# Attention halves exchanged by DMA and rotated on GpSimd, keys copied twice out of PSUM, and one modulation unit folded earlier

## The reference

```python
def ffn_sublayer(x, shift, scale, gate, g_pre, g_post, w_in, w_out):
    h = modulate(rmsnorm(x, g_pre), shift, scale)
    a, b = jnp.split(h @ w_in, 2, axis=-1)
    h = (jax.nn.silu(a) * b) @ w_out
    return x + FFN_RES * gate * rmsnorm(h, g_post)

def apply_rope(x, cos, sin):
    x1, x2 = jnp.split(x, 2, axis=-1)
    return jnp.concatenate([x1 * c - x2 * s, x1 * s + x2 * c], axis=-1)

# attention, 16 query heads of 64 on 4 key heads; rope on the latent tokens alone
q, k, v = attn_project(h, w_qkv)           # context: softmax(q k) v with a sink
q, k = apply_rope(q, cos, sin), apply_rope(k, cos, sin)   # latent
# latent queries see a window of latent keys, the cached keys and the sink
```

## Time and profile before

| | us |
|---|---|
| median of 3 runs (lowest, highest) | 3009.32 (3008.97, 3010.02) |
| the profiled execution, whole | 3009.04 |
| its span, first to last instruction | 3007.2 |
| PE busy | 2956.2 (98%) |
| DVE busy | 2209.8 (73%) |
| ACT busy | 1152.2 (38%) |
| POOL busy | 561.6 (19%) |
| DMA rate | 172 GB/s mean |

### The profile page before, as it was taken

The page is one execution under the profiler, slowest core; times in us unless marked ns, Lnnn a source line. Parts: engine busy times, 40 slices in busy tenths (PEclk is TensorE's granted clock), DMA queues, the critical chain, the costliest instruction groups (busy, mean ns, idle before and its releaser), DMA issues.

```text
span 3007.2 us, 46610 instructions
## 1 busy us (share of the span) xinstructions
PE 2956.2 (98%) x18194; PEld 2749.9 (91%) x18194; DVE 2209.8 (73%) x2897; ACT 1152.2 (38%) x1966; POOL 561.6 (19%) x586
## 2 busy tenths in 40 slices
PE   7999999999999999999999999999999999999999
PEld 6999889999999998999899999979999999889998
DVE  6888678887987657888888576768888888775444
ACT  4222664223322424222422365553224222664222
POOL 1111112112111112111211144631112111211001
PEclk9999999999999999999999999999999999999999
DMA  9667445665665445766566443337675766333443
GB/s 306 211 215 215 140 91 187 212 211 170 217 213 175 119 128 173 223 213 199 178 213 201 134 118 104 95 99 231 211 216 181 220 212 197 112 81 114 127 128 95
DMA packets 589696, 517.76 MB, mean 172 GB/s; under 512 B 66773, under 2 KB 523046, under 8 KB 587686
## 3 DMA queue, kind: packets, MB, share of 16 engines
q1 hardware_dynamic: 588918, 514.53, 56.6%
q10 hardware_dynamic: 560, 0.25, 0.0%
...
## 4 chain that ended last, share of the span: by engine, by line
PE 91%; issue 4%; DVE 2%; POOL 1%; ACT 1%; DMA 1%; SPq 0%; DVEq 0%; POOLq 0%; another core or an unknown queue 0%; ACTq 0%
PE bank L1698 19%; PE bank L1700 19%; PE bank L1699 19%; PE bank L1752 9%; PE bank L1751 9%; PE bank L1750 9%; PE bank L1725 1%; PE bank L619 1%; PE bank L1715 1%; PE bank L644 1%; DVE h_hi L2266 1%; DMA ada_first<-w_ada 1%; DVE h_lo L2276 0%; POOL hg_kr L1497 0%; PE bank L1783 0%
## 5 line engine op out<-in xcount | busy, mean ns | idle before, releaser
L1698 PE MATMUL bank<-h_hi,w_hi 128*128 128x384 f32 x3328 | 1120.6, 337 | 0.0
L1700 PE MATMUL bank<-h_hi,w_lo 128*128 128x384 f32 x3328 | 1114.6, 335 | 0.0
L1699 PE MATMUL bank<-h_lo,w_hi 128*128 128x384 f32 x3328 | 1113.8, 335 | 0.0
L1947 ACT ACTIVATE w_hi<-raw 128x1024 fp32r<-128x1024 f32 x646 | 681.1, 1064 | 1020.1 <-PE bank L1700 481.6
L2109 DVE TENSOR_TENSOR w_lo<-raw,w_hi 128x1024 fp32r<-128x1024 f32 x648 | 810.4, 1274 | 310.9 <-ACT w_hi L1947 305.7
L1698 PEld LDWEIGHTS bank<-h_hi,w_hi 128*128 128x128 f32 x3328 | 625.3, 188 | 10.9 <-ACT tmp L1966 1.6
L1699 PEld LDWEIGHTS bank<-h_lo,w_hi 128*128 128x128 f32 x3328 | 625.4, 188 | 6.1
L1700 PEld LDWEIGHTS bank<-h_hi,w_lo 128*128 128x128 f32 x3328 | 625.2, 188 | 0.0
L2136 DVE SCALAR_TENSOR_TENSOR fold<-ada_raw,cond,fold 128x1024 f32<-128x1024 f32 x462 | 616.4, 1390 | 0.1
L2455 POOL TENSOR_TENSOR h_lo<-tmp,h_hi 128x384 fp32r<-128x384 f32 x176 | 250.2, 1421 | 1762.9 <-DVE h_hi L2180 1762.9
L1752 PE MATMUL bank<-w_hi,h_lo 128*128 128x512 f32 x1056 | 414.0, 392 | 0.0
...
## 6 DMA issues: line engine op xcount, KB each, us to landing
...
```

Source lines behind the costliest of these rows:

```text
L1698: mm(out, wh, h_hi[:, k, :], start=(k == 0), stop=False)
L1699: mm(out, wh, h_lo[:, k, :], start=False, stop=False)
L1700: last = mm(out, wl, h_hi[:, k, :], start=False, stop=(k == DC - 1))
L1947: A(w_hi[:, b % RING, :], raw[:, b % RAW, :], ACT.Copy).then_inc(w_hi_made, 1)
```

## The change

1. **Rope.** `rotate` is gone. SP copies the halves across partitions by DMA from `qkv` or `kd` into one of four buffers (`rope_tmp` twice, `rope_more` twice): two DMAs for a key head, four for a query chunk. POOL then multiplies the copy by the sine, the original by the cosine, and adds. DVE has no part in rope.
2. **Keys.** `dup` and the `take` of the key blocks are gone. ACT (block 0) and DVE (block 1) copy each key head twice from PSUM into `kd`, and the 128 context columns into `qkv`.
3. **Order.** The second value block moves to the end of the input blocks; its transposes run in the last loop step. Scores of chunk 2 and of chunk 7 stand earlier in their loop step. The exchanges stand in SP's list at blocks 8, 13 and 14 to 19.
4. **Unit 7** is folded in feed-forward 0, so that it holds six units in 22 steps of two or three slabs. Its sum is written at block 8 and spread at block 9 of the first attention, and its `mod_fold` stands in the loop step j = 0 there. The PE work and the loads of this unit in the attention are gone.
5. Slabs of feed-forward 0 are loaded two blocks later, its sums spread three blocks later; the constant table of an attention shrinks from 2048 to 1408 columns; the first eight slabs share semaphores in pairs.

```diff
-    QKV_CHUNKS = [DC, DC + 1, 0, DC + 2, DC + 3] + list(range(1, DC))
+    QKV_CHUNKS = [DC, DC + 1, 0, DC + 2] + list(range(1, DC)) + [DC + 3]
...
-    units_of = {0: (2, 7), 1: (7, 8), 2: (8, 13), 3: (13, 17), 4: (17, 17), 5: (17, 22), 6: (22, 26), 7: (26, 26),
+    units_of = {0: (2, 8), 1: (8, 8), 2: (8, 13), 3: (13, 17), 4: (17, 17), 5: (17, 22), 6: (22, 26), 7: (26, 26),
                 8: (26, 31), 9: (31, 36), 10: (36, 36), 11: (36, 36)}
     units_end = [units_of[s][1] for s in range(12)]
-    FOLD_F = 4
+    UNIT_STARTS = {5: (0, 4, 8, 12, 16, 20), 6: (0, 4, 8, 11, 15, 18, 21)}
...
     def sums_of(s):
         u0, u1 = units_of[s]
-        return {FOLD_F * (u - u0 + 1): u for u in range(u0, u1)}
+        return {unit_starts(s)[u - u0 + 1]: u for u in range(u0, u1)}
     def mods_of(s):
-        return {f + 2: u for f, u in sums_of(s).items()}
+        return {f + (4 if s == 0 else 2): u for f, u in sums_of(s).items()}
     def left_over(s):
...
     def spreads_of(s):
-        return {at_a(f) + 11: u for f, u in sums_of(s).items()}
+        return {at_a(f) + (14 if s == 0 else 11): u for f, u in sums_of(s).items()}
     def slabs_at(s, f):
-        u0, u1 = units_of[s]
-        u = u0 + f // FOLD_F
-        return [(u, 2 * (f % FOLD_F) + n) for n in range(2)] if u < u1 else []
+        starts = unit_starts(s)
+        for i, u in enumerate(range(*units_of[s])):
+            length = starts[i + 1] - starts[i]
+            if starts[i] <= f < starts[i + 1]:
+                per = -(-DC // length)
+                first = per * (f - starts[i])
+                return [(u, k) for k in range(first, min(first + per, DC))]
+        return []
...
-    attn_k = place("attn_k", [P, 5 * P + 2 * TS + KEYS], F32, x_end - 2 * D * 4)
+    attn_k = place("attn_k", [P, 2 * TS + KEYS], F32, x_end - 2 * D * 4)
...
+    rope_more = place("rope_more", [P, 2, TS], F32, x_end - 2 * TS * 4)
+    rope_of = [rope_tmp[:, 0, :], rope_tmp[:, 1, :], rope_more[:, 0, :], rope_more[:, 1, :]]
+    ROPE_BUFFERS = len(rope_of)
...
-    ROPE_ORDER = [("k", 0), ("k", 1), ("q", 0), ("k", 2), ("k", 3)] + [("q", j) for j in range(1, DC)]
-    FIRST_ROPES = 5
-    Q_AT = {j: ROPE_ORDER.index(("q", j)) for j in range(DC)}
+    TAKES = len(QKV_CHUNKS) - 2
+    FIRST_BLOCKS = 5
+    ROPE_ORDER = [("k", 0), ("k", 1), ("q", 0), ("k", 2), ("q", 1), ("k", 3)] + [("q", j) for j in range(2, DC)]
+    FIRST_ROPES = 6
+    ROPE_AT = {x: n for n, x in enumerate(ROPE_ORDER)}
+    KEY_SWAPS, QUERY_SWAPS = {8: (0, 1, 3), 13: (5,)}, {8: 2, 13: 4} | {b: b - 8 for b in range(14, 20)}
...
+    def rope_place(n):
         kind, i = ROPE_ORDER[n]
         return kd[:, i, TP:T] if kind == "k" else qkv[:, i, TP:T]
+    def swap_runs(n):
+        if ROPE_ORDER[n][0] == "k":
+            return [(0, 32, 96), (96, 0, 32)]
+        return [(to, to ^ 32, 32) for to in range(0, P, 32)]
...
+    def copy_keys(copy, c):
+        rows = [slice(0, HD), slice(HD, P)]
+        copy(qkv[:, DC + c, 0:TP], psum[c][:, 0:TP])
+        for x in range(2):
+            for half in rows:
+                last = copy(kd[half, 2 * c + x, :], psum[c][rows[x], 0:T])
+        return last
...
-            pe.wait_ge(rope_add, ROPE * a + Q_AT[j] + 1)
-            pe.wait_ge(k_dup_copied, KVH * a + g + 1)
+            pe.wait_ge(rope_add, ROPE * a + max(ROPE_AT["q", j], ROPE_AT["k", g]) + 1)
...
         in_block(b0 + 2, qkv_bank(2))
         turn_cache()
-        dup(0)
-        pe.wait_ge(qkv_taken, taken + 1)
-        rotate(0)
-        rotate(1)
         for u in units:
             unit_half(u, 0)
         in_block(b0 + 3, qkv_bank(3))
-        dup(1)
-        rotate(2)
-        dup(2)
-        rotate(3)
         for u in units:
             unit_half(u, 1)
-        pe.wait_ge(qkv_taken, taken + 1)
         in_block(b0 + 4, qkv_bank(4))
         for u in units:
             ada_turn(u, 1)
-        dup(3)
-        rotate(4)
-        pe.wait_ge(mods_made, units_end[s])
+        if units:
+            pe.wait_ge(mods_made, units_end[s])
         scores(0)
         for j in range(DC - 1):
-            pe.wait_ge(rope_sin, ROPE * a + FIRST_ROPES + j - (1 if j == 0 else 0))
-            in_block(b0 + FIRST_ROPES + j, 7)
+            pe.wait_ge(qkv_taken, taken + take_number(FIRST_BLOCKS + j - 1))
+            in_block(b0 + FIRST_BLOCKS + j, 7)
             if j == 0:
                 turn_values()
             else:
                 turn_probs(2 * j - 2)
-            rotate(FIRST_ROPES + j)
+            if j in (1, DC - 2):
+                if j == DC - 2:
+                    turn_last_values()
+                scores(j + 1)
             if j >= 2:
                 values(j - 2)
             if j >= 1:
                 turn_probs(2 * j - 1)
-            scores(j + 1)
+            if j not in (1, DC - 2):
+                scores(j + 1)
...
-        take(0)
-        take(1)
+        act.wait_ge(block_done, b0 + 1)
+        copy_keys(lambda dst, src: A(dst, src, ACT.Copy), 0).then_inc(k_copied[0], 1)
         split(b0 + 6)
         split(b0 + 7)
         take(2)
         copy_cache()
...
-        copy_key(1)
-        copy_key(2)
         split(b0 + 9)
...
+            if j == DC - 2:
+                copy_last_values()
...
+        dve.wait_ge(block_done, b0 + 2)
+        copy_keys(lambda dst, src: V.tensor_copy(dst, src), 1).then_inc(k_copied[1], 1)
         split(b0 + 6)
         split(b0 + 7)
-        rope(0)
-        rope(1)
         split(b0 + 8)
-        rope(2)
-        rope(3)
         split(b0 + 9)
-        add_left_over()
+        add_left_over(0)
         for u in range(*units_of[s]):
             ada_add(2 * u + 1, 1)
             mod_add(u, 1)
-        rope(4)
...
             normalize(2 * j)
-            rope(FIRST_ROPES + j)
             split(b0 + 10 + j)
             if j >= 1:
                 copy_probs(2 * j - 1)
             normalize(2 * j + 1)
+            if j == 0:
+                add_left_over(1)
...
-        def cosine(n):
-            kind, i = ROPE_ORDER[n]
-            gp.wait_ge(rope_rot, ROPE * a + n + 1)
-            if kind == "k":
-                gp.wait_ge(k_dup_copied, KVH * a + i + 1)
-            G.tensor_tensor(rope_dst(n), rope_dst(n), cos_t, ALU.mult).then_inc(rope_cos, 1)
+        def rope(n):
+            gp.wait_ge(rope_swapped[n % ROPE_BUFFERS], swaps_made(a, n))
+            G.tensor_tensor(rope_of[n % ROPE_BUFFERS], rope_of[n % ROPE_BUFFERS], sin_t, ALU.mult).then_inc(rope_sin, 1)
+            G.tensor_tensor(rope_place(n), rope_place(n), cos_t, ALU.mult).then_inc(rope_cos, 1)
+            gp.wait_ge(rope_sin, ROPE * a + n + 1)
+            gp.wait_ge(rope_cos, ROPE * a + n + 1)
+            G.tensor_tensor(rope_place(n), rope_place(n), rope_of[n % ROPE_BUFFERS], ALU.add).then_inc(rope_add, 1)
...
+        def swap(s, n):
+            a, (kind, i) = attn_number(s), ROPE_ORDER[n]
+            if kind == "k":
+                sp.wait_ge(k_copied[i // 2], a + 1)
+            else:
+                sp.wait_ge(qkv_taken, TAKES * a + take_number(QKV_CHUNKS.index(i)))
+            need(sp, rope_add, ROPE * a + n + 1 - ROPE_BUFFERS)
+            for to, of, rows in swap_runs(n):
+                sp.dma_start(rope_of[n % ROPE_BUFFERS][to:to + rows, :], rope_place(n)[of:of + rows, :]
+                             ).then_inc(rope_swapped[n % ROPE_BUFFERS], 16)
...
+                if sub_kind[s] == "attn":
+                    for n in KEY_SWAPS.get(b, ()):
+                        swap(s, n)
                 if s > 0 or b >= 4:
                     load_block(b0 + b)
+                if sub_kind[s] == "attn" and b in QUERY_SWAPS:
+                    swap(s, QUERY_SWAPS[b])
...
-                        slabs.setdefault(at_a(f) + 3 + n, []).append(slab)
+                        slabs.setdefault(at_a(f) + (5 if s == 0 else 3) + n, []).append(slab)
...
-                pe.wait_ge(ada_first_in[4 * half + n], 16)
+                pe.wait_ge(first_in(4 * half + n), 32 if half < 2 else 16)
```

131 lines of the change are left out of this document (52 added, 79 removed).

## The result

The changed kernel takes 3027.18 us (median of 4 runs, 3023.59 to 3028.84), the kernel before 3009.14 beside it (3006.22 to 3010.02). The ratio is 1.0059, its 95% interval 1.0045 to 1.0073: some 18 us slower, where 9 us less were forecast. The profiled execution took 3027.79 us, its span is 3026.0 against 3007.2.

A forecast was written before the change was run, and what follows sets the result against it. PE was taken to bound the kernel, busy 2956.2 of 3007.2 us. Gains of 8.8 us (second attention) and 3.4 (first), less 3.0 (feed-forward 0), made 9.2 off 3009.0: 2999.8 us, range 2988 to 3009.

The forecast's parts named there:

- The clock: First attention, behind the long wait for chunk 1's rope: 1 us charged for the clock.
- The order at the end of the attention: Both attentions: the order of transposes and scores moves, their number doesn't; no cost was given.
- The chain of the first exchanges: Start of the second attention: PE waits 0.9 us at scores(0) and 1.4 us at scores(1) for POOL's rope.
- the rule: First three ropes: DVE and POOL block each other a whole instruction; gain some 7 us smaller, by the rows about 2.
- SP's wait for the modulation and chunk 1's exchange: First attention: SP waits for unit 6's modulation, chunk 1 comes late; PE waits 9.4 us instead of 1.4, 8.0 lost.
- Feed-forward 0: Late in feed-forward 0: sixteen more folds and a sum on DVE make PE wait; 3.0 us lost, ends 0.5 and 7.
- The steady exchanges: Loop iterations of the attentions: each exchange has 11 us of room, needs at most 8.1 us, and hides.
- B: Unit 7 costs more than it gives: 7 us in feed-forward 0, 3 us more by SP's wait; 3007 us, chance 0.17.
- C: Exchange slow everywhere: 15 us in ten iterations, 14 before scores(0) and scores(1) of each attention; 3029 or 3014, chance 0.11.

The follow-up runs named there:

- e9: The changed kernel with scores(7) put back behind values(4) and turn_probs(11), where it stood before: 3015.84 us.
- e5: The changed kernel with the exchange of query chunk 1 moved from behind block 13 to behind block 10 in SP's list: 3017.53 us.
- e10: The changed kernel with the three short intervals of feed-forward 0's modulation units at its beginning instead of in its second half: 3013.03 us.
- e1: The kernel before with only unit 7 folded in feed-forward 0, the attentions otherwise as they were: 3015.38 us.
- e6: The changed kernel with one DMA of 128 partitions per query chunk instead of four of 32, query halves not exchanged: 3013.74 us.
- e14: The changed kernel with SP's write of the gains moved from right behind the last exchange to behind the stores of new keys and values: 3017.24 us.
- e4: The kernel before with only the keys copied twice from PSUM by ACT and DVE, the rotation staying on PE: 3003.19 us.
- e13: The changed kernel with the edits of e5, e9 and e10 together: 2998.11 us.

## Why the prediction was wrong, step by step

**The clock (mis-sized, the largest single term).** I charged 1 us for one long wait. Six stretches at the half clock cost 15.0 us, 12.1 without the one that a later wait would have taken anyway. A wait of 2.7 us was followed by 2.9 us of it in the first attention. The row I took the 1 us from, transposes that last 1.97 instead of 1.09, shows only the first few instructions behind a pause; I should have read how long the half clock goes on. The Trainium skill, "TensorE: Matmul & The Clock Gate", section "HAM oscillation — how this bites in real kernels", describes a kernel that falls back to the slow clock at every wait for a DMA and pays the return each time. These rows agree in part: here the waits are for POOL, DVE and ACT, and six of the seven of 2.6 us and more were paid for so.

**The order at the end of the attention (costed at nothing).** I wrote that the order of the transposes and scores moves, their number doesn't. With scores(7) ahead of values(4) nothing is left between the second transposes and the next, which wait for ACT's copy: 3.13 us in the second attention, 0.78 in the first, where scores(7) also stands 6.22 us before work that was ready. e9 shows that the order is worth 11 us here, 7.5 of them in the first attention and 3.1 in the second.

**The chain of the first exchanges (right mechanism, 2 us short).** Chunk 0's rope was to end 13.75 us after block 2's start and ended at 15.7, so PE waited 2.62 instead of 0.9. The six key DMAs and chunk 0's four left 0.7 us later than forecast, since one takes some 0.6 us of SP and not 0.33 to 0.43. The rope took 3.3 us instead of 2.3. Scores(1) of the second attention waited 3.47 where 1.4 was worked out: the four DMAs of its exchange left until 2626.06, 2.2 us later than forecast, and landed 3.4 to 4.3 us after their issues, where I had taken 1.8 to 2. The timeline of DVE and of POOL, first attention:
```profile
348.19 1.42 DVE L2119 TENSOR_TENSOR w_lo<-raw,w_hi 128x1024 fp32r<-128x1024 f32 x1 [4.11 <-ACT w_hi L1957]
352.00 1.50 DVE L2119 TENSOR_TENSOR w_lo<-raw,w_hi 128x1024 fp32r<-128x1024 f32 x1 [2.40 <-ACT w_hi L1957]
```
```profile
347.79 0.74 POOL L887 TENSOR_TENSOR kd<-kd,rope_tmp 128x256 f32<-128x256 f32 x1
348.48 1.70 POOL L883 TENSOR_TENSOR rope_more<-rope_more,attn_k 128x256 f32<-128x256 f32 x1
...
352.37 1.72 POOL L884 TENSOR_TENSOR kd<-kd,attn_k 128x256 f32<-128x256 f32 x1
```
A step that meets a split takes 1.50 to 1.72 us against 0.73, six times in the two attentions' first ropes taken together. I had taken 0.2 to 0.6 a meeting from before's single row and left the price of the rule to a sentence. The rule of the Trainium skill, "SBUF — State Buffer", section "Who interferes with whom", that the two engines block each other for a whole instruction, came nearer.

**SP's wait for the modulation and chunk 1's exchange (right place, over-sized, with luck in the number).** SP stood until 354.19 behind block 9 and sent this exchange at 360.45. PE waited 7.91 us, where 9.4 was worked out. The two are close by luck: the rope ended 33.3 us behind block 2's start and not 29.8, since the halves landed 4.1 to 4.7 us after their issues, and PE came 5.1 us later than worked out, held up at scores(0) and by the half clock behind it. e5 and e10 confirm the place. But with SP free, in e10, PE still waits 4.84 us, so SP's wait is worth some 3 us of the 7.9 and not the 8.0 that I charged.

**Feed-forward 0 (right place, half the price, and the wait came by another way).** I worked out 3.0 us of waiting near the end from the time that DVE's folds take, and the last block waited 4.06; the half clock behind it, 2.5, was not in the sum. DVE's six folds of step 19 took 7.25 us, within what I gave them. Then DVE itself stood idle for 3.56 us, for ACT's rounding of a weight block, and ACT had waited 9.02 us for that block, which landed 15.0 us after its issue. The rows of SP, ACT and DVE:
```profile
280.27 3.42 SPq L1553 DMA_DIRECT2D raw<-w_ffn_out  x1
295.28 1.06 ACT L1957 ACTIVATE w_hi<-raw 128x1024 fp32r<-128x1024 f32 x1 [9.02 <-DMA raw<-w_ffn_out]
296.37 1.23 DVE L2119 TENSOR_TENSOR w_lo<-raw,w_hi 128x1024 fp32r<-128x1024 f32 x1 [3.56 <-ACT w_hi L1957]
```
In e1, e5, e6, e9 and e14, which have the same order of units, DVE idles 2.0 to 3.7 us there and PE waits 2.5 to 4.2, always 0.5 more. So the term that I left out is the late weight block: SP, held by DVE's folds, sends it at 280.27, where it left at 275.4 before and landed in 7.9 us. e10 shows what would have avoided it: this block and the next leave at 274.7 and 276.5 and PE waits for neither, though they land only 12.0 and 13.0 us later.

**The steady exchanges (right).** Chunks 2 to 6 were never waited for in the changed kernel, and an iteration takes 9.45 us instead of 9.97. The copies of the keys hide as well: e4.

**The rivals.** B had the sign of the unit's part: alone it costs 7.6 us. C had the size, but only half of its mechanism: no iteration of the steady part waits (15 of its 29 us), while its 14 us more ahead of the first scores came as waits of 10.6 and 6.1 us at scores(0) and scores(1), where before had 1.3 and 2.4, and the half clock behind them. No rival held that a half clock follows such waits, nor the order at the end. That the sum was not far off for the work is shown by e13: the same parts in other places take 2998.
